# Expert blocks in a hybrid diffusion step: four 32-row tiles of mixed experts a block, against one expert a block with its weights as the stationary operand

## The reference, cut to what matters

```python
sh1, sc1, g1, sh2, sc2, g2 = split(silu(c) @ w_mod + b_mod, 6)       # w_mod 1024 x 6144
h = rms_norm(x, norm1) * (1 + sc1) + sh1
u, q, k, v = split(h @ w_in)                                          # 1024 x 1536
mix = concat([fourier_mixer(u), windowed_attention(q, k, v, sink)])
x = x + g1 * (mix @ w_out)
h = rms_norm(x, norm2) * (1 + sc2) + sh2
idx, gate = top-8 of 64 experts for each token (4 of 8 groups first, sigmoid scores)
routed = sum over the 8 of gate * ((silu(h @ w_gate[e]) * (h @ w_up[e])) @ w_down[e])   # 1024x256, 1024x256, 256x1024
x = x + g2 * (routed + shared_expert(h))
y = rms_norm(x, norm_f)
```

## Time and profile before

| what | value |
|---|---|
| median of three runs | 1085.35 us (1082.56 to 1085.72) |
| profiled execution | 1084.15 us, span from first to last instruction 1082.3 us |
| mean granted TensorE clock | 0.988 of full speed |
| PE busy | 1022.1 us (94%) |
| DVE, ACT, POOL busy | 330.1, 231.6, 164.2 us |
| DMA | 321.64 MB, 297 GB/s mean |
| gate/up matmuls (L1964) | 3264 instructions, 468.6 us |
| down matmuls (L1984) | 1632 instructions, 239.3 us |
| chain that ended last | PE 74%, DMA 13%, DVE 5%, SP's queue 5% |

### The profile page before, as it was taken

One profiled execution on the slowest core, in us unless ns is written; L12 is line 12 of the kernel. 1 busy time (PEld: TensorE's weight loads), 2 busy tenths in 40 slices (PEclk: granted clock), 3 DMA queues, 4 the chain that ended last, 5 costly groups with the idle time before them and its releaser, 6 DMA issues.

```text
span 1082.3 us, 18470 instructions
## 1 busy us (share of the span) xinstructions
PE 1022.1 (94%) x7328; PEld 459.7 (42%) x7328; DVE 330.1 (30%) x825; ACT 231.6 (21%) x545; POOL 164.2 (15%) x238
## 2 busy tenths in 40 slices
PE   6999998999999999999999999999899999999574
PEld 2655556565455553334333333434333334333121
DVE  0112226764246763111121111121111112111177
ACT  1211106664123221111111111111111112111011
POOL 1000010300321111112122112122121121210000
PEclk9999999999999999999999999999999999999798
DMA  9964409300401657599999999999999999995596
GB/s 375 404 246 155 156 31 267 142 1 1 175 39 54 254 211 251 211 351 423 363 395 418 416 420 421 421 421 419 421 411 396 421 417 422 421 419 214 228 409 265
DMA packets 60222, 321.64 MB, mean 297 GB/s; under 512 B 10308, under 2 KB 10956, under 8 KB 32104
## 3 DMA queue, kind: packets, MB, share of 16 engines
q1 hardware_dynamic: 43184, 272.71, 62.9%
q0 software_dynamic: 14816, 43.34, 10.3%
q10 hardware_dynamic: 2136, 4.39, 1.1%
HBM read 299.86 MB, written 32.44 MB: 307 GB/s over the span
## 4 chain that ended last, share of the span: by engine, by line
PE 74%; DMA 13%; DVE 5%; SPq 5%; ACT 2%; issue 1%; POOL 0%; POOLq 0%; DVEq 0%; ACTq 0%
PE bank L1964 29%; PE bank L1984 14%; PE bank L1559 8%; DMA ring<-in_w_up 7%; PE bank L1731 5%; PE bank L1936 4%; DMA ring<-expert_rows 3%; PE bank L1823 3%; PE bank L1756 2%; PE bank L1742 1%; PE bank L1715 1%; PE bank L1829 1%; PE bank L1586 1%; DMA ring<-in_w_mod 1%; PE bank L1836 1%
## 5 line engine op out<-in xcount | busy, mean ns | idle before, releaser
L1964 PE MATMUL bank<-ring,reg_h 128*32 128x512 f32 x2592 | 333.1, 594 | 0.6 <-DMA ring<-in_w_up 0.4
L1964 PEld LDWEIGHTS bank<-ring,reg_h 128*32 128x32 f32 x2592 | 100.9, 110 | 181.1 <-issue 181.0
L1984 PE MATMUL bank<-ring,reg_y 128*32 128x512 f32 x1296 | 170.6, 594 | 1.5 <-ACT reg_y L989 1.5
L1964 PE MATMUL bank<-reg_p,reg_h 128*32 128x512 f32 x672 | 135.5, 598 | 3.8 <-DMA ring<-in_w_up 3.8
L1431 DVE TENSOR_TENSOR reg_h<-reg_p,bank 128x256 f32<-128x256 f32 x51 | 21.5, 421 | 338.4 <-ACT reg_p L1007 325.3
L704 POOL DMA_INDIRECT expert_rows<-reg_y,rowc x51 | 51.2, 1005 | 270.2 <-DVE reg_y L1415 258.4
L1007 ACT ACTIVATE reg_p<-bank 128x256 f32<-128x256 f32 x51 | 19.6, 384 | 322.5 <-PE bank L1964 322.5
L1559 PE MATMUL bank<-ring,reg_h 128*128 128x384 f32 (+2 forms) x256 | 84.3, 487 | 0.0
L1984 PEld LDWEIGHTS bank<-ring,reg_y 128*32 128x32 f32 x1296 | 47.5, 110 | 82.6 <-issue 78.6
L1415 DVE TENSOR_SCALAR reg_y<-bank,reg_p 128x512 f32<-128x512 f32 x51 | 38.3, 750 | 143.8 <-PE bank L1984 143.8
L1731 PE MATMUL bank<-ring,reg_h 128*128 128x512 f32 x160 | 70.3, 594 | 0.0
(11 more groups left out here) (269 smaller groups left out, 948.2 us busy)
## 6 DMA issues: line engine op xcount, KB each, us to landing
ring<-in_w_gate SPq DMA_DIRECT2D x51, 1024.0 KB
ring<-in_w_up SPq DMA_DIRECT2D x51, 1024.0 KB
ring<-in_w_down SPq DMA_DIRECT2D x51, 1024.0 KB, 17.6
ring<-in_w_mod SPq DMA_DIRECT2D x21, 1024.0 KB, 8.3
ring<-expert_rows SPq DMA_DIRECT2D x19, 1024.0 KB, 16.2
reg_p<-in_w_gate SPq DMA_DIRECT2D x13, 1024.0 KB
reg_p<-in_w_up SPq DMA_DIRECT2D x13, 1024.0 KB
reg_p<-in_w_down SPq DMA_DIRECT2D x13, 1024.0 KB
```

The lines of the kernel that those rows point to most:

```text
L1964: last = pe.matmul(bank[2 + p][R * j:R * j + R, :], xg_t[:, p, k * P + R * j:k * P + R * j + R], w_gu(homes[n % SLOTS])[:, k], start=(k == ...
L1984: last = pe.matmul(bank[5 + hf][R * j:R * j + R, :], h_t[:, p, i * P + R * j:i * P + R * j + R], w_dn(homes[n % SLOTS])[:, i, 512 * hf:512 ...
```

## The change

An expert's rows no longer share a block with another's. Each rank gets blocks of 128 rows of its own: six ranks (3 to 8, `WIDE`) two, all others one. The order is again mixed. Gate and up swap operands: the weights are the stationary operand (128x128 pieces), and the block's 128 tokens are streamed, so that gate and up come out with the features on the partitions and h needs no transposes (`hh`, `block_h`, `h_t_out` go). Down loads h (128x128) and streams 512 columns over the whole array. PE's order in a block is gate/up of b, transposes of b + 2, down of b. The down matrix is laid out as two rows of 4 KB a partition. The tables of places shrink with the number of different places.

Besides: the biases of the second and third modulation group are loaded by ACT into the places of the copies and added by DVE; the first two later pieces move behind the first half of projection tile 1; the Fourier map uses bank 5 in place of bank 2, with its order and waits adapted; `shared_down(2)` stands ahead of the first block's transposes.

```diff
-UNITS = (4,) * FIXED + (5,) * 6 + (4,) * 15 + (3,) * 22 + (2,) * 18
-ORDER = tuple(range(FIXED)) + tuple(FIXED + (i // 2 if i % 2 == 0 else E - FIXED - 1 - i // 2) for i in range(E - FIXED))
-FIRST = tuple(sum(UNITS[r] for r in ORDER[:n]) for n in range(E))
-TILES = tuple((n, u) for n, r in enumerate(ORDER) for u in range(UNITS[r]))
-NQ = len(TILES) // 4
-LAST = tuple((FIRST[n] + UNITS[r] - 1) // 4 for n, r in enumerate(ORDER))
-XGROUPS = 14
+DOUBLE = 6
+WIDE = tuple(range(FIXED, FIXED + DOUBLE))
+LARGE = tuple(range(FIXED + DOUBLE, FIXED + DOUBLE + (E - FIXED - DOUBLE) // 2))
+SMALL = tuple(range(E - 1, LARGE[-1], -1))
+def expert_order():
+    order = list(range(FIXED)) + [r for pair in zip(SMALL, LARGE + (None,)) for r in pair if r is not None]
+    step = (E - FIXED) // DOUBLE
+    for i, r in enumerate(WIDE):
+        order.insert(FIXED + 4 + step * i, r)
+    return tuple(order)
+ORDER = expert_order()
+BLOCKS = tuple(2 if r in WIDE else 1 for r in ORDER)
+FIRST = tuple(sum(BLOCKS[:n]) for n in range(E))
+EXPERT = tuple(n for n in range(E) for _ in range(BLOCKS[n]))
+NQ = len(EXPERT)
+LAST = tuple(FIRST[n] + BLOCKS[n] - 1 for n in range(E))
+XGROUPS = 9
...
-            for n in range(SLOTS, E + 1):
-                if n < E:
-                    e[n] = sp.value_load(eid[0:1, n:n + 1], min_val=0, max_val=E - 1)
-                    sp.wait_ge(s_g, LAST[n - SLOTS] + 1)
-                    load_gate_up(n, e[n])
-                if n > SLOTS:
-                    sp.wait_ge(s_y, LAST[n - 1 - SLOTS] + 1)
-                    load_down(n - 1, e[n - 1])
+            for n in range(SLOTS, E):
+                e[n] = sp.value_load(eid[0:1, n:n + 1], min_val=0, max_val=E - 1)
+                sp.wait_ge(s_g, LAST[n - SLOTS] + 1)
+                load_gate_up(n, e[n])
+                sp.wait_ge(s_y, LAST[n - SLOTS] + 1)
+                load_down(n, e[n])
...
+            def down_rows_of(e):
+                return wd_v[e] if isinstance(e, int) else wd_v[bass.ds(e, 1)].rearrange("e p k n -> (e p) k n")
             def load_down(n, e):
-                sp.dma_start(homes[n % SLOTS][:, 4096:SLOT], rows_of(wd_v, e)).then_inc(s_dn[n % SLOTS], 16)
+                sp.dma_start(w_dn(homes[n % SLOTS]), down_rows_of(e)).then_inc(s_dn[n % SLOTS], 16)
...
-            for b in range(0, NQ, 2):
-                if b:
-                    next_scatter(b - 2)
-                    next_scatter(b - 1)
+            for b in range(NQ):
...
-                next_gather(b + 5)
-            next_scatter(NQ - 1)
+                next_scatter(b)
...
+            act.wait_ge(s_clr, 5)
+            for q in range(1, 3):
+                for j in range(4):
+                    act.dma_start(mod_rows[q][R * j:R * j + 2, :],
+                                  b_mod[0:1, 2048 * q + 512 * j:2048 * q + 512 * j + 512].to_broadcast([2, 512])).then_inc(s_bias, 16)
...
-            for b in range(0, NQ, 2):
-                if b:
-                    y_out(b - 2)
-                silu(b, 0)
-                if b:
-                    y_out(b - 1)
-                if b + 1 < NQ:
-                    silu(b + 1, 1)
-                h_t_out(b, 0)
-                for n in range(b + 2, min(b + 4, NQ)):
-                    xt_half(n, n % 2, bank[xt_banks(n)[0]])
-                if b + 1 < NQ:
-                    h_t_out(b + 1, 1)
-            y_out(NQ - 1)
+            for b in range(NQ):
+                silu(b, b % 2)
+                if b + 2 < NQ:
+                    xt_half(b + 2, b % 2)
+                y_out(b)
...
                 dve.wait_ge(s_mpe, KD * (q + 1))
-                dve.tensor_copy(mod_rows[q], bank[(0, 0, 1)[q]][:, :]).then_inc(s_mrow, 1)
+                if q:
+                    dve.wait_ge(s_bias, 8 * 16)
+                    dve.tensor_tensor(mod_rows[q], mod_rows[q], bank[q - 1][:, :], ALU.add).then_inc(s_mrow, 1)
+                else:
+                    dve.tensor_copy(mod_rows[q], bank[0][:, :]).then_inc(s_mrow, 1)
...
-                at_least(dve, s_ht, b - 1)
-                dve.tensor_tensor(hh[:, p, :], sg[:, p, :], bank[2 + p][:, F:2 * F], ALU.mult).then_inc(s_h, 1)
+                at_least(dve, s_y, b - 1)
+                dve.tensor_tensor(h_t[:, p, :], sg[:, p, :], bank[2 + p][:, F:2 * F], ALU.mult).then_inc(s_h, 1)
...
-            for b in range(0, NQ, 2):
-                if b:
-                    y_out(b - 2)
-                gated(b, 0)
-                if b:
-                    y_out(b - 1)
-                if b + 1 < NQ:
-                    gated(b + 1, 1)
-                for n in range(b + 2, min(b + 4, NQ)):
-                    x_in(n)
-            y_out(NQ - 1)
+            for b in range(NQ):
+                gated(b, b % 2)
+                if b + 2 < NQ:
+                    x_in(b + 2)
+                y_out(b)
...
-            def mod_bias(q):
+            def mod_bias():
...
-                    pe.matmul(bank[(0, 0, 1)[q]][R * j:R * j + R, :], ident[0:12, 4 * q + j:4 * q + j + 1].to_broadcast([12, R]),
-                              b_rows, start=True, stop=False)
+                    pe.matmul(bank[0][R * j:R * j + R, :], ident[0:12, j:j + 1].to_broadcast([12, R]), b_rows,
+                              start=True, stop=False)
...
-                                     start=False, stop=(k == KD - 1))
+                                     start=(q > 0 and k == 0), stop=(k == KD - 1))
...
                     projection(t, (0, 1))
+                    if t == 1:
+                        later_pieces(0)
                     later_pieces(2 * t - 1)
...
                     qk_t(t - 1)
-                if t < T - 1:
+                if 0 < t < T - 1:
                     later_pieces(2 * t)
...
-                    last = pe.matmul(bank[2][:, 0:wn], m_cs[:, x, n // 2, :], y_cs[n % 2][:, x, 0:wn], start=(x == 0), stop=(x == 1))
+                    last = pe.matmul(bank[5][:, 0:wn], m_cs[:, x, n // 2, :], y_cs[n % 2][:, x, 0:wn], start=(x == 0), stop=(x == 1))
...
+            fourier_y(2)
...
-            fourier_y(2)
...
-                    if p:
-                        pe.wait_ge(s_fo, 4)
...
+                    elif b:
+                        pe.wait_ge(s_fo, 4)
...
-            pe.matmul(bank[7][:, 0:4 * NQ], rank_e.to_broadcast([E, P]), tiles[:], start=True, stop=True)
-            pe.matmul(bank[7][:, 4 * NQ:4 * NQ + XBLK], x_e.to_broadcast([P, P]), ident[:, 0:XBLK], start=True, stop=True)\
+            pe.matmul(bank[7][:, 0:NQ], rank_e.to_broadcast([E, P]), tiles[:], start=True, stop=True)
+            pe.matmul(bank[7][:, NQ:NT], x_e.to_broadcast([P, P]), ident[:, 0:XBLK], start=True, stop=True)\
...
-            def block_transposes(b, p, gathered, banks=(0, 1)):
+            def block_transposes(b, p, gathered):
...
+                at_least(pe, s_xa, b)
+                at_least(pe, s_xb, b)
...
-                    last = pe.transpose(bank[banks[k // 4]][:, (k % 4) * P:(k % 4 + 1) * P], v[:, k, :], ident)
+                    last = pe.transpose(bank[k // 4][:, (k % 4) * P:(k % 4 + 1) * P], v[:, k, :], ident)
...
-            def x_in(b):
-                if xt_banks(b)[0] == 5:
-                    at_least(pe, s_ya, b - 2)
-                    at_least(pe, s_yb, b - 2)
-                block_transposes(b, b % 2, 16 * (b // 2 + 1), xt_banks(b))
-            def block_h(cb, p):
-                pe.wait_ge(s_h, cb + 1)
-                at_least(pe, s_he, cb)
-                h_transposes(hh[:, p, :]).then_inc(s_ht, 1)
-            def block_gate_up(b):
-                p = b % 2
-                tiles = [n for n, u in TILES[4 * b:4 * b + 4]]
-                pe.wait_ge(s_xa, b + 1)
-                pe.wait_ge(s_xb, b + 1)
-                at_least(pe, s_h, b - 1)
-                for n in sorted(set(tiles)):
-                    if FIRST[n] >= 4 * b:
-                        pe.wait_ge(*gate_up_in(n))
-                for k in range(KD):
-                    for j, n in enumerate(tiles):
-                        last = pe.matmul(bank[2 + p][R * j:R * j + R, :], xg_t[:, p, k * P + R * j:k * P + R * j + R],
-                                         w_gu(homes[n % SLOTS])[:, k], start=(k == 0), stop=(k == KD - 1))
+            def block_gate_up(b, p, home):
+                w = w_gu(home)
+                for i in range(2):
+                    for j in range(2):
+                        out = bank[2 + p][:, (2 * i + j) * P:(2 * i + j + 1) * P]
+                        for k in range(KD):
+                            last = pe.matmul(out, w[:, k, i, j * P:(j + 1) * P], xg_t[:, p, k * P:(k + 1) * P],
+                                             start=(k == 0), stop=(k == KD - 1))
...
-            def block_down(b):
-                p = b % 2
-                tiles = [n for n, u in TILES[4 * b:4 * b + 4]]
-                pe.wait_ge(s_he, b + 1)
+            def block_down(b, p, home):
+                pe.wait_ge(s_h, b + 1)
...
-                if b % 2 == 0:
```

(71 more changed lines are left out.)

41 lines of the change are left out of this document (16 added, 25 removed).

## The result

The kernel after takes 1306.89 us (median of four runs, 1306.51 to 1307.73), the one before 1085.53 us (median of four, on the same chip): a ratio of 1.2046, 95% interval 1.2022 to 1.2070. It is slower by 221 us; the forecast was 1304, range 1284 to 1332. The profiled execution has a span of 1304.8 us at a mean clock of 0.991.

The account below looks back on a forecast made before the run. PE was taken as the expert stage's first bound, transfers close behind. The profiled 1084.15 us, plus 223 for 70 blocks of 11.74 us (822 against 599), less 3.4 for small edits, gave 1304 us, range 1284 to 1332.

Parts of the forecast that it names:

- The main term: Expert stage on PE: 70 blocks of 11.74 us, 822 us against 599, so +223 us.
- The wait with its restart: PE between gate/up and down of one block: exposed wait for h, 0.30 us a block, bounds 0.1 and 0.7.
- The saving on the transposes of h and the mode changes: Expert stage on PE: these go, since h comes out with features on the partitions; 0.34 us a block saved.
- loads not fully hidden: Rival, gate/up: 128-column loads not hidden under 128 moving columns, 0.128 us an instruction, 1380 us in all; 8%.
- Transfers: Expert stage: 201 MB of weights plus 43 MB of rows at 298 GB/s, share 0.71, with PE as the bound.
- Small edits: Outside the main expert work: several small changes, together -3.4 us.
- (a): Projections: DVE adds later modulation groups' biases in its copy; the third group's instructions, about 1.0 us, come off PE.
- (b): Projection tile 1: second group's biases and first two pieces leave the place before it; projection starts at 57.4, not 59.14.
- (c): Start of attention: Fourier map writes another bank, so scores(1) needn't wait for ACT's copy; -1.4 us, bounds 0 and -2.
- (d): First gather: shared_down(2) ahead of the first block's transposes fills PE's 1.14 us wait; -1.2 us.
- faster or the same: Rival, expert stage: transfers set the pace, 1065 us, if gate/up takes under 0.061 us an instruction; 1%.

Follow-up runs that it names:

- experiment 7: The kernel before with the small edits alone (modulation biases, moved pieces, Fourier map's bank, `shared_down(2)` earlier): 1082.72 us, ratio 0.9977.
- experiment 3: The kernel after with down of block b - 1 done after gate/up of b and the transposes of b + 2: 1285.03 us, ratio 1.1839.
- experiments 4 and 5: The kernel after with gate and up streaming 64 of a block's 128 tokens, 1307.76 us; and the layout kernels of experiment 5.
- experiment 5: Kernel after, 8 KB down rows: every second column loaded 1336.74 us, side by side 1309.83; every sixteenth element 1779.05. Kernel before, 4 KB down rows: 1087.54.

## Why the prediction was right

*The main term.* 70 blocks of 11.74 were forecast, 70 of 11.79 came: stage 822 against 825.5. By runs the 221 us split along the kernels above: +212.3 for the 19 blocks in the old form (1085.5 to 1297.8), -12.8 for the swapped operands with the small edits (to 1285.0), +21.9 for down right behind gate and up (to 1306.9). Of the 12.8, 2.7 are the small edits by experiment 7 and 10.5 are 70 times the 0.15 us below.

*Its parts.* Gate and up 7.10 against 7.14; transposes 0.89 against 0.88; down with the wait 3.75 against 3.77. The wait with its restart was 0.30 against 0.33, and experiment 3 took it away. The saving on the transposes of h and the mode changes was 0.34, and down saves 0.08 more (3.44 for the mean of 3.61 and 3.43); in the same order of work a net 0.15 is left, since gate and up cost 0.27 more than in the old form (7.14 for 6.87). So the forecast got the block within 0.05 us part by part, and not by errors that cancel.

*The rival "loads not fully hidden".* Its numbers didn't come, but its thought was nearer than I gave it credit: the loads are what sets the pace (experiments 4 and 5), and they happen to need 0.111 us, about the streaming time of 128 columns. I took the agreement of the two for a sign that the load hides under the columns. Here the size was right and its reason was not, and that the two lie so close was luck. The Trainium skill's rule ("TensorE: Matmul & The Clock Gate", "LDWEIGHTS (loading the stationary operand)"), columns over 1.2 whatever the rows, gives 107 ns for the load. The runs show a pace of 111 ns side by side and of 118 and 217 with steps, with load records of 192, 196 and 312 ns; the step of what is loaded has no place in the rule.

*What the sum left out.* The layout of what PE loads. I treated the layouts as a question of transfers alone, and there the answer held: nothing that shows in this kernel, and 2 us in the kernel before, about 4 with what the same edit gave back on the transposes of h. That the columns lie side by side is worth 27 us in this kernel, and without it the time would have been 1336.7 (experiment 5), 33 us above the forecast and just outside its range.

*Transfers.* Hidden, as forecast; without the weights' fetch the stage is as long. The two numbers under it were off. The rate was 278 GB/s and not 298: my 245 MB counted the first five experts' 15.7 MB, which had come before the stage. In it 230 MB were moved (278 GB/s by 825.5 us), as many as before (384 by 598.9). The share was 0.77 and not 0.71, although fewer bytes would give less. The packets rose from 60,222 to 73,923: 8,192 of them by the halved rows of down, 5,472 by POOL's queue, from 14,816 to 20,288 at the same 43.4 MB (19 more gathers and 19 more scatters, 144 packets each, for rows that mostly hold nothing). Neither accounts for the share. With the weights' fetch left out it is 0.23 of 595 us with 51 blocks and 0.16 of 824 us with 70, the same 130 to 140 us. And the weights' own queue took 62.9% of the span of 1082.3 before, 681 us, but 56.2% of 1307.9, 735 us, in experiment 5's kernel with 8 KB rows, at the same 43,184 packets; 4 KB rows made it 748 (57.3% of 1304.8). Why the same packets take some 54 us longer in a longer stage stays open.

*Small edits.* -3.4 forecast, -2.7 measured with an interval of -3.4 to -1.5. The profile of experiment 7 shows 0.9 us for the 0.8 of (a) and (b), 0.85 for (c)'s 1.4 and 0.03 for (d)'s 1.2, together 1.8. (d) failed in its mechanism: it filled one wait and opened another as long.

*The side of "faster or the same"* needed 0.061 us an instruction. No run came near it.

## What to carry to other kernels

When a block's cost doesn't depend on how full it is, count blocks first: two kernels with the same work and nearly the same time a block (11.61 and 11.79 us) differ by 20% because one pads to 32 rows and the other to 128. Swapping the operands so that the weights stand still doesn't make a thin block cheaper, since the load of 128 columns then sets the pace; it pays only in what follows (no transposes of h). And when the load sets the pace, lay out what is loaded side by side, and put more than the hand-over's length of other work (here 1.14 us, where the transposes filled 0.88) between a product and the step that needs its result from two other engines.

## What the runs showed of the hardware that I had not expected

- 64 moving columns on a 128x128 load take as long as 128: 8.02 us with the transposes behind them, both times, on 32-bit data in two instructions a product.
- For products, a load of every second element takes 196 ns for 192 and makes the pace 5% slower; of every sixteenth 312 ns and 94% slower (7.53 and 13.87 us a block for 7.14).
- For transposes, a step of two makes the load 204 ns for 141 (experiment 5, the kernel before), a step of eight 188 for 140, and the pace at a step of eight stays at 0.110 us. Why a transpose's load is shorter than a product's to begin with was not tried, and stays open.
- Indirect transfers of a block issue the same number of packets, 144 each, however few of its rows are valid. Their time on the DMA engines didn't grow with the 19 further blocks: 0.23 of 595 us and 0.16 of 824 us in the kernels without the weights' fetch.
